# Normalised rows and squares in free PSUM banks, one root for the double norm, and the last chunks in token halves, in a two-block fp32 kernel on Trainium2

## The reference

```python
u = _modulate(h, g_ffn[l], sh2, sc2)                       # norm, scale, shift
h = h + gt2[:, None, :] * _conv_ffn(u, w_up[l], w_conv[l], b_conv[l], w_down[l])
return _rmsnorm(h, g_final)                                 # end of the first block
...
h = _rmsnorm_2(x, norm_g)                                   # start of the second
p = h @ w_in
(u, v, z_a, x_b, b_g, c_g, z_b, x_c, z_c, g_a, g_b, g_c) = jnp.split(p, _split_points(), axis=-1)
...
return x + merged @ w_o                                     # x is the once-normed row
```

## Time and profile before

| | us |
|---|---|
| median of 3 runs (lowest, highest) | 2197.65 (2197.61, 2199.75) |
| the profiled execution | 2197.53 |
| its span, first to last instruction | 2195.8 |
| outside the span | 1.7 |
| PE busy in the span | 2140.2 (97%) |
| DVE, ACT, POOL busy | 797.5, 415.8, 1048.4 |

### The profile page before, as it was taken

The page is one execution under the profiler, slowest core; times in us unless marked ns, Lnnn a source line. Parts: engine busy times, 40 slices in busy tenths (PEclk is TensorE's granted clock), DMA queues, the critical chain, the costliest instruction groups (busy, mean ns, idle before and its releaser), DMA issues.

```text
span 2195.8 us, 25443 instructions
## 1 busy us (share of the span) xinstructions
PE 2140.2 (97%) x10478; PEld 1782.1 (81%) x10478; DVE 797.5 (36%) x1072; ACT 415.8 (19%) x575; POOL 1048.4 (48%) x451
## 2 busy tenths in 40 slices
PE   7999999999999899999999989999999999999997
PEld 3788888888888788888888788888888888888885
DVE  6961355545543621222222674310031111331232
ACT  3202323233421310201111331111000110110102
POOL 1538447554453345445363525435545446435550
PEclk9999999999999999999999999999999999999999
DMA  9545554554451102011111221102111011101131
GB/s 347 118 101 153 192 149 144 155 153 136 167 182 39 39 31 85 29 48 48 48 58 29 87 106 58 38 30 67 58 39 48 29 58 58 48 29 58 38 124 77
DMA packets 157117, 192.26 MB, mean 88 GB/s; under 512 B 11152, under 2 KB 138720, under 8 KB 157024
## 3 DMA queue, kind: packets, MB, share of 16 engines
q1 hardware_dynamic: 148096, 172.05, 25.3%
q10 hardware_dynamic: 8928, 18.88, 2.3%
HBM read 159.20 MB, written 31.70 MB: 87 GB/s over the span
## 4 chain that ended last, share of the span: by engine, by line
PE 93%; DVE 3%; POOL 1%; DMA 1%; issue 1%; ACT 0%; SPq 0%; DVEq 0%; POOLq 0%; ACTq 0%
PE ps L718 62%; PE ps L792 8%; PE ps L740 8%; PE ps L750 4%; PE ps L1014 3%; PE ps L975 2%; PE ps L905 1%; PE ps L989 1%; DVE act_l L1797 1%; PE ps L1137 1%; POOL w_h L639 1%; DVE nrm L1786 1%; DMA ada_w<-in_w_ada 1%; PE ps L1242 1%; POOL w_l L641 1%
## 5 line engine op out<-in xcount | busy, mean ns | idle before, releaser
L639 POOL TENSOR_SCALAR w_h<-raw 128x1024 fp32r<-128x1024 f32 (+2 forms) x202 | 506.6, 2508 | 934.7 <-PE ps L718 595.5
L718 PE MATMUL ps<-act_h,w_h 128*128 128x512 f32 x1568 | 613.2, 391 | 1.0 <-POOL w_l L641 0.6
L718 PE MATMUL ps<-act_l,w_h 128*128 128x512 f32 x1568 | 610.6, 389 | 0.0
L718 PE MATMUL ps<-act_h,w_l 128*128 128x512 f32 x1568 | 610.6, 389 | 0.0
L641 POOL TENSOR_TENSOR w_l<-raw,w_h 128x1024 fp32r<-128x1024 f32 (+2 forms) x202 | 436.9, 2163 | 16.9
L718 PEld LDWEIGHTS ps<-act_h,w_h 128*128 128x128 f32 x1568 | 294.7, 188 | 65.9 <-issue 2.9
L718 PEld LDWEIGHTS ps<-act_h,w_l 128*128 128x128 f32 x1568 | 294.6, 188 | 61.4
L718 PEld LDWEIGHTS ps<-act_l,w_h 128*128 128x128 f32 x1568 | 294.8, 188 | 61.0 <-issue 0.5
L718 PE MATMUL ps<-in_h,w_h 128*128 128x512 f32 x384 | 150.3, 391 | 0.0
L718 PE MATMUL ps<-in_l,w_h 128*128 128x512 f32 x384 | 150.1, 391 | 0.0
L718 PE MATMUL ps<-in_h,w_l 128*128 128x512 f32 x384 | 150.1, 391 | 0.0
(11 more groups left out here) (325 smaller groups left out, 2824.2 us busy)
## 6 DMA issues: line engine op xcount, KB each, us to landing
raw<-in_w_in SPq DMA_DIRECT2D x45, 1024.0 KB, 5.2
raw<-in_w_up SPq DMA_DIRECT2D x16, 1024.0 KB, 5.5
ada_w<-in_w_ada SPq DMA_DIRECT2D x8, 1024.0 KB, 11.9
ada_lo<-in_w_ada SPq DMA_DIRECT2D x16, 512.0 KB, 3.9
ada_hi<-in_w_ada SPq DMA_DIRECT2D x16, 512.0 KB, 4.8
gates_scratch<-gate_st ACTq DMA_DIRECT2D x32, 256.0 KB, 2.5
gate_in<-gates_scratch SPq DMA_DIRECT2D x16, 512.0 KB, 4.5
raw<-in_w_down SPq DMA_DIRECT2D x16, 512.0 KB, 3.5
```

Source lines behind the costliest of these rows:

```text
L639: nc.gpsimd.tensor_scalar(w_h[:, k, c, :], src[:, c, :], 1.0, None, ALU.mult).then_inc(s["w_high"], 1)
L718: last = nc.tensor.matmul(dst[:, tok], w[:, k, kw + c, P * cg:P * cg + P], x[:, c, tok], start=(c == 0 and p == 0), stop=(c == kc - 1 and ...
```

## The change

**First norm.** The first half's sums go into the middle of u 0 (after its fourth input chunk), its spread into u 1 (after the third). The normalised rows' two buffers are now PSUM banks of slots 1 and 2, and the squares of chunks 4 to 7 are written into the PSUM banks from which the same chunk's product has just been read. ACT's root comes before the square of chunk 4's second half, and a dummy root (`root_table`) ahead of the squares. DVE does its second-half residuals and adds inside the loop of the first half's norm. The up-chunks go one at a time: slot 0, the second half's sums, slot 1 with the spread inside, slot 2, then slots 0, 1, 2 of the second half, and slot 3 whole.

**Double norm.** Four down chunks are whole and four (u 4 to 7) go in halves. ACT squares once, and the second sum is made on DVE by a multiply-add with `final_sq`. From both sums one root gives the product of the two reciprocals directly (`eps_sq`), and a second root, of the first norm alone, is spread later. The first half's sums stand after u 4 of the second half and its spread after u 5, with u 6 and u 7 behind it. The normalised rows go to PSUM banks (in the second half only the even chunks), and the squares of chunks 4 to 7 too. The first rows product of block two now takes one weight block at a time, with four token tiles per chunk; it waits until `sq_used` is past chunk 6's second half, since it overwrites the bank of that square. `scaled_out` comes behind both norms.

```diff
-        product_half(slot(u), 1 - u // 2, u % 2, KD, act_h, act_l, th)\
+        after = {}
+        if th and u == 0:
+            after[3] = lambda: statistics(acc, 7, slot(0)[:, 0:4], 0)
+        if th and u == 1:
+            after[2] = lambda: everywhere(2, slot(3)[:, 0:HALF], diag_a[:, 0]).then_inc(s["rstd_ready"], 1)
+        product_half(slot(u), 1 - u // 2, u % 2, KD, act_h, act_l, th, after=after)\
             .then_inc(s["gemm"] if th else s["first_half"], 1)
-        if th and u == 0:
-            statistics(acc, 7, slot(0)[:, 0:4], 0)
-        if th and u == 1:
-            everywhere(2, slot(3)[:, 0:HALF], diag_a[:, 0]).then_inc(s["rstd_ready"], 1)
...
-pair_half((0, 1), 1, 0, U_FFN, lambda: statistics(acc, 11, slot(2)[:, HALF:HALF + 4], 1))
-everywhere(3, slot(3)[:, HALF:T], diag_a[:, 1]).then_inc(s["rstd_ready"], 1)
+product_half(slot(0), 1, 0, KD, act_h, act_l, 0, each=s["u_ready"], base=U_FFN)
+statistics(acc, 11, slot(3)[:, HALF:HALF + 4], 1)
+product_half(slot(1), 1, 1, KD, act_h, act_l, 0, after={
+    4: lambda: everywhere(3, slot(3)[:, 0:HALF], diag_a[:, 1]).then_inc(s["rstd_ready"], 1)})
 split_done(N_FFN + 1)
-for cg in range(2):
-    product_half(slot(2 + cg), 0, cg, KD, act_h, act_l, 0)
-pair_half((0, 1), 1, 1, U_FFN + KD)
-for cg in range(2):
-    product_half(slot(2 + cg), 0, cg, KD, act_h, act_l, 1).then_inc(s["gemm"], 1)
+product_half(slot(2), 0, 0, KD, act_h, act_l, 0)
+product_half(slot(0), 1, 0, KD, act_h, act_l, 1, each=s["u_ready"], base=U_FFN + KD).then_inc(s["gemm"], 1)
+product_half(slot(1), 1, 1, KD, act_h, act_l, 1).then_inc(s["gemm"], 1)
+product_half(slot(2), 0, 0, KD, act_h, act_l, 1).then_inc(s["gemm"], 1)
+product(slot(3), 0, 1, KD, act_h, act_l).then_inc(s["gemm"], 1)
...
-down(None, 3, KD - 2)
+down(None, 3, 4)
 for th in range(2):
-    for u in (6, 7):
+    for u in range(4, KD):
+        n = 8 * 3 + N_FFN + 4 + u // 2
+            if u % 2 == 0:
+                pe.wait_ge(s["w_half"], n + 1)
+        product_half(slot(u % 4), 1 - (u // 2) % 2, u % 2, 4, in2_h, in2_l, th,
+                     rest=None if th or u % 2 else n).then_inc(s["gemm"] if th else s["first_half"], 1)
+        if th and u == 4:
+            both_sums(0, slot(0))
+        if th and u == 5:
+            spread(4, slot(1)[:, 0:HALF], diag_b[:, 0])
...
+pe.wait_ge(s["w_half"], N_V2 + 1)
+    if c == 0:
+        pe.wait_ge(s["sq_used"], SQ_DOWN + 4 * 2 * 2 + 5)
+    for t in range(4):
+        last = rows_tile(0, 0, t, c)
+    if c == 4:
+        both_sums(1, slot(3)[:, HALF:T])
+last.then_inc(s["gemm"], 1)
+split_done(N_V2 + 1)
+for t in range(4):
+    for c in range(KD):
+        last = rows_tile(0, 1, t, c)
+    if t == 0:
+        spread(6, slot(3)[:, HALF:T], diag_a[:, 0])
+        spread(5, slot(1)[:, 0:HALF], diag_b[:, 1])
+        spread(7, slot(1)[:, HALF:T], diag_a[:, 1])
+last.then_inc(s["gemm"], 1)
+pe.wait_ge(s["rstd1_read"], 2)
...
-    if c >= 3:
-        act.wait_ge(s["sq_used"], c + 2 if th and c >= 6 else c - 2)
-    A.activation(sq[:, c % 2, tok] if c else acc[:], h_t[:, c, tok], ACT.Square).then_inc(s["sq_ready"], 1)
+    if c == 3:
+        act.wait_ge(s["sq_used"], 1)
+    dst = acc[:] if c == 0 else sq[:, c % 2, :] if c < 4 else slot(c % 4)[:, tok]
+    A.activation(dst, h_t[:, c, tok], ACT.Square).then_inc(s["sq_ready"], 1)
...
+root_table()
 for c in range(4):
     square(c)
 for c in range(4, KD):
     square(c, 0)
+root(1, 0, slot(0)[:, 0:4])
 square(4, 1)
-root(1, 0, slot(0)[:, 0:4])
-square(5, 1)
-norm_high(U_FFN, slice(0, HALF), lambda i: nrm[:, i, 0:HALF], shift_ffn, lambda: square(6, 1))
+norm_high(U_FFN, slice(0, HALF), lambda i: slot(1 + i)[:, 0:HALF], shift_ffn,
+          {3: lambda: square(5, 1), 6: lambda: square(6, 1)})
 square(7, 1)
-root(2, 1, slot(2)[:, HALF:HALF + 4])
-norm_high(U_FFN + KD, slice(HALF, T), lambda i: nrm[:, i, HALF:T], shift_ffn)
+root(2, 1, slot(3)[:, HALF:HALF + 4])
+norm_high(U_FFN + KD, slice(HALF, T), lambda i: slot(1 + i)[:, HALF:T], shift_ffn)
...
+    act.wait_ge(s["down_read"], AHEAD + 24 + c + 1 + (4 if th else 0))
+    if c == 3:
+        act.wait_ge(s["sq_used"], SQ_DOWN + 3)
+    dst = acc2[:, 0, :] if c == 0 else sq[:, c % 2, :] if c < 4 else slot(c % 4)[:, tok]
+    A.activation(dst, h_t[:, c, tok], ACT.Square).then_inc(s["sq_ready"], 1)
...
+def roots(th):
+    cols = slice(4 * th, 4 * th + 4)
+    for m, (row, eps) in enumerate(((0, eps_sq), (3, eps_rms))):
+        act.wait_ge(s["ms2_ready"], 2 * th + 2)
+        A.activation(stat[:, row, cols], stat[:, 2 if m else 0, cols], ACT.Sqrt, scale=1.0 / D, bias=eps[:])\
+         .then_inc(s["std_ready"], 1)
...
+first_buf = [slot(1)[:, HALF:T], slot(3)[:, 0:HALF]]
+second_buf = [slot(3)[:, 0:HALF], sq[:, 1, 0:HALF]]
+root_table()
+for c in range(4):
+    square2(c)
+for c in range(4, KD):
+    square2(c, 0)
+square2(4, 1)
+roots(0)
+square2(5, 1)
+norm_high(U_IN2, slice(0, HALF), lambda i: first_buf[i], None,
+          {1: lambda: square2(6, 1), 3: lambda: square2(7, 1)})
+roots(1)
+norm_high(U_IN2 + KD, slice(HALF, T), lambda i: second_buf[i], None,
+          {1: lambda: keep_rstd(0, 6, slot(1)[:, 0:HALF]), 3: lambda: keep_rstd(1, 7, slot(1)[:, HALF:T])})
...
-    v.tensor_tensor(acc[:, tok], acc[:, tok], sq[:, c % 2, tok], ALU.add).then_inc(s["sq_used"], 1)
+    src = sq[:, c % 2, tok] if c < 4 else slot(c % 4)[:, tok]
+    v.tensor_tensor(acc[:, tok], acc[:, tok], src, ALU.add).then_inc(s["sq_used"], 1)
...
-residual(4, 1)
 one_over_root(2, slice(0, 4))
 on_diagonal(diag_a[:, 0], stat[:, 1, 0:4])
-residual(5, 1)
+residual(4, 1)
 add_square(4, 1)
 dve.wait_ge(s["rstd_ready"], 2)
-norm(U_FFN, slice(0, HALF), lambda i: nrm[:, i, 0:HALF], gain[:, 1], shift_ffn, slot(3)[:, 0:HALF], second_half)
+norm(U_FFN, slice(0, HALF), lambda i: slot(1 + i)[:, 0:HALF], gain[:, 1], shift_ffn, slot(3)[:, 0:HALF],
+     {2: lambda: residual(5, 1), 3: lambda: add_square(5, 1), 5: lambda: residual(6, 1), 6: lambda: add_square(6, 1)})
 residual(7, 1)
-add_square(6, 1)
 add_square(7, 1)
 one_over_root(3, slice(4, QB))
 on_diagonal(diag_a[:, 1], stat[:, 1, 4:QB])
 dve.wait_ge(s["rstd_ready"], 3)
-norm(U_FFN + KD, slice(HALF, T), lambda i: nrm[:, i, HALF:T], gain[:, 1], shift_ffn, slot(3)[:, HALF:T])
+norm(U_FFN + KD, slice(HALF, T), lambda i: slot(1 + i)[:, HALF:T], gain[:, 1], shift_ffn, slot(3)[:, 0:HALF])
...
-    for u in range(KD - 2 if last else KD):
+    for u in range(4 if last else KD):
+        if last and u == 1:
+            dve.wait_ge(s["sq_ready"], 13)
+            v.tensor_scalar(acc2[:, 1, :], acc2[:, 0, :], final_sq[:, 0:1], None, ALU.mult).then_inc(s["sq_used"], 1)
         if last and u >= 2:
             add_squares(u - 1)
...
+    n = c + (4 if th else 0)
+    src = sq[:, c % 2, tok] if c < 4 else slot(c % 4)[:, tok]
+    dve.wait_ge(s["sq_ready"], 12 + n + 1)
+    dve.wait_ge(s["sq_used"], SQ_DOWN + 2 * n - 1)
+    v.tensor_tensor(acc2[:, 0, tok], acc2[:, 0, tok], src, ALU.add).then_inc(s["sq_used"], 1)
+    v.scalar_tensor_tensor(acc2[:, 1, tok], src, final_sq[:, c:c + 1], acc2[:, 1, tok], ALU.mult, ALU.add)\
+     .then_inc(s["sq_used"], 1)
...
+def sums_out(th, src):
+    dve.wait_ge(s["sums_ready"], 4 + 2 * th)
+    v.tensor_copy(stat[:, 2, cols], src[:, 0:4]).then_inc(s["ms2_ready"], 1)
+    dve.wait_ge(s["ms2_ready"], 2 * th + 1)
+    v.scalar_tensor_tensor(stat[:, 0, cols], stat[:, 2, cols], RMS_EPS, src[:, 4:8], ALU.mult, ALU.add)\
+     .then_inc(s["ms2_ready"], 1)
+def both_diagonals(th, d):
+    cols = slice(4 * th, 4 * th + 4)
+    dve.wait_ge(s["std_ready"], 4 + 2 * th)
+    step(v.reciprocal(stat[:, 1, cols], stat[:, 0, cols]))
+    on_diagonal(d[:, 0], stat[:, 1, cols])
+    dve.wait_ge(s["std_ready"], 5 + 2 * th)
     step(v.reciprocal(stat[:, 4, cols], stat[:, 3, cols]))
-    step(v.tensor_tensor(stat[:, 5, cols], stat[:, 4, cols], r1, ALU.mult))
-    on_diagonal(d[:, 1], stat[:, 5, cols])
+    on_diagonal(d[:, 1], stat[:, 4, cols])
...
+step(v.tensor_tensor(gain2[:], col_b("g_final", 0, KD), col_b("norm_g_2", 0, KD), ALU.mult))
+step(v.tensor_tensor(final_sq[:], col_b("g_final", 0, KD), col_b("g_final", 0, KD), ALU.mult))
...
+residual2(4, 0)
+add_squares(3)
+for c in range(5, KD):
+    residual2(c, 0)
+    add_squares(c - 1, 0)
 add_squares(7, 0)
-residual2(6, 1)
-both_norms(0, 4, 4, slot(0)[:, HALF:HALF + 4], diag_b)
+residual2(4, 1)
+sums_out(0, slot(0))
+add_squares(4, 1)
+both_diagonals(0, diag_b)
+residual2(5, 1)
+add_squares(5, 1)
+dve.wait_ge(s["sq_used"], SQ_DOWN + 2 * 9 + 1)
+dve.wait_ge(s["rstd_ready"], 4)
+first_buf = [slot(1)[:, HALF:T], slot(3)[:, 0:HALF]]
+second_buf = [slot(3)[:, 0:HALF], sq[:, 1, 0:HALF]]
+norm(U_IN2, slice(0, HALF), lambda i: first_buf[i], gain2, None, slot(1)[:, 0:HALF],
+     {0: lambda: residual2(6, 1), 1: lambda: add_squares(6, 1),
+      2: lambda: residual2(7, 1), 3: lambda: add_squares(7, 1)})
+sums_out(1, slot(3)[:, HALF:T])
+both_diagonals(1, diag_a)
 dve.wait_ge(s["rstd_ready"], 5)
```

(9 more changed lines are left out.)

166 lines of the change are left out of this document (47 added, 119 removed).

## The result

| | before | after |
|---|---|---|
| median (lowest, highest), us | 2197.63 (2195.18, 2199.75) | 2179.51 (2174.77, 2180.25) |
| profiled execution, its span | 2197.53, 2195.8 | 2179.59, 2177.9 |
| PE busy in the span | 2140.2 (97%) | 2134.9 (98%) |

The ratio is 0.9913, with a 95% interval of 0.9896 to 0.9931: 18.1 us faster between the medians, where 19.3 were forecast.

The account below looks back on a forecast made before the run. PE, busy for 97% of the span, bounds the kernel, so only its idle and slow time can be won. Gains of 7.9 and 11.4 make 19.3 us off 2197.53: 2178.2, median 2178.3, range 2175.5 to 2181.5 (0.62).

Parts of the forecast that it names:

- The total: Both norms: gains of 7.9 and 11.4 make 19.3 us off the profiled execution, median 2178.3 us.
- First norm: First norm: 8.2 us of idle and slow PE time recovered, less a wait of 0.3, gains 7.9 us.
- Double norm: Double norm: 19.1 us recoverable, less new waits and slow clock of 1.3, 1.5, 0.15, 3.2 and 1.5, gains 11.4.
- 1.3 forecast for the weights: Double norm: PE idles 1.3 us for the weights of u 6 and 7, which POOL splits by 1236.6.
- 1.5 at the sums: Double norm, after u 4: PE idles 1.5 us before the sums, until DVE's adds are done at 1245.1.
- 3.2 ahead of the rows product: Double norm: PE idles 3.2 us until chunk 6's adds free the square's bank; slow clock then costs 1.5 us.
- Rival (a): Double norm: clock also falls in the two gaps before the sums, 8 us apart; 2181.5 to 2185, chance 0.14.
- PSUM operands: DVE in both norms: PSUM operands taken at equal price, 0.75 us; up to 0.1 more each would give 2181.
- rival (d): Both norms, slower: scalings that write PSUM and read their factor there cost 1.1 us extra each; 2204, chance 0.03.
- Rival (b): Both norms: POOL still stops DVE, the cause not being the second SBUF input; gains 2.5 and 9, 2186, chance 0.09.
- a DVE operation does not stand still for a TENSOR_SCALAR: DVE beside POOL: operations with both inputs in SBUF stall for POOL's TENSOR_TENSOR only; `act_l` beside a `w_h` took 0.75.
- The table load: First norm: the 1.28 us load moves ahead of the squares; root, reciprocal and diagonal then end at 698.6.

Follow-up runs that it names:

- rows_in_sbuf: Changed kernel with the buffers of the normalised rows back in SBUF in both norms, squares and order as changed: 2188.15 us, 8.6 above the changed kernel.
- combined_late: Changed kernel with the edits of squares23_psum and square6_sbuf, plus chunk 6's and 7's adds and the second sums two chunks later: 2174.76 us, again 2175.91.
- squares23_psum: Changed kernel with the squares of chunks 2 and 3 of the double norm also in PSUM: 2175.69 us, ratio 0.99.
- the probes: Changed kernel with idle gaps and sums put into PE's stream in block two, alone, paired or together; one profiled execution, no total time given.
- square6_sbuf: Changed kernel with the second half of chunk 6's square in SBUF, not in the bank the rows product overwrites: 2180.01 us, ratio 0.9919.
- no_early_table: Changed kernel without the two dummy roots ahead of the squares, in both norms: 2177.95 us, ratio 0.9908.
- first_norm_only: Kernel before the change with only the first norm's hunks, its double norm as it was: 2190.82 us, ratio 0.9967.
- double_norm_only: Kernel before the change with only the double norm's hunks, its first norm as it was: 2186.95 us, ratio 0.9948.
- combined_v2: combined_late with the first half's sums one input chunk later and chunk 6's second residual ahead of the third scaling: 2174.0 us, ratio 0.9892.

## Why the prediction was right, point by point

**The total** holds: 19.3 us forecast for the two norms, 8.35 + 10.95 = 19.3 measured. That the two agree to a tenth is luck: the gaps of the double norm came out 1.2 us shorter than forecast, and a slow stretch of 1.7 us that the sum did not have came in. (The list of waits has a line of 6.5 us between the two that I read as the longest; it is PE's wait for the input at the start, outside the norms.)

**First norm, 7.9 forecast, 8.35 measured.** The steps came as drawn: sums inside u 0, spread 5.7 us after them, no stall in `act_l`, the second half's adds ready at 720.91 where PE reached the sums at 724.19, so 3.3 us of slack. I had put a wait of 0.2 to 0.3 at chunk 7 of the second half; there is none: the norm's last `act_l` ends at 741.39, and PE runs through. `rows_in_sbuf` shows that the PSUM buffers carry 6.2 of the 8.35.

**Double norm, 11.4 forecast, 10.95 measured.** The gaps: 1.3 forecast for the weights (its terms, 1236.6 and 1235.4, give 1.2), 0.86 measured; 1.5 at the sums, 1.19 measured (each chunk's residual and adds repeat after 1.92 us, not 1.98); 0.15 at the spread, none measured; 3.2 ahead of the rows product, 2.86 measured. Behind that gap the clock fell as forecast. The term that was missing is the slow clock at the sums: from their start to the next matmul it took 2.11 us (1237.64 to 1239.75) and the 12 matmuls behind took 4.14 (to 1243.89), where 1.80 (`combined_late`, 1236.09 to 1237.89) and 2.72 are the prices at the upper level: 1.7 us lost. Rival (a), with a chance of 0.14, had such a loss at 1.5 to 3.5. Its total of 2181.5 to 2185 did not come, since the gaps made up for most of it: 4.91 us against the 6.15 forecast. Its reason, that two gaps lie 8 us apart, is not borne out: in `squares23_psum` the first gap is gone and the clock fell at the sums, and the probes' pair of gaps left it at 1.00.

**PSUM operands** cost nothing, as taken: 0.76 against 0.75 for a scaling into PSUM, 0.68 for an add from PSUM and 0.68 for one from SBUF (before, at 683.47), and ACT's square into PSUM takes 0.60 where it took 0.63 into SBUF. That excludes rival (d). The rule of the Trainium skill, "VectorE: DVE Perf Modes", section on the TRN2 errata, on a dearer PSUM source, is not seen here.

**Rival (b)**, that POOL stops DVE for another reason, is excluded by `rows_in_sbuf`, `square6_sbuf` and `squares23_psum`: one input moved to SBUF brings 0.74 up to 2.9, one input moved to PSUM takes 2.3 down to 1.28. In all thirteen profiles 127 SCALAR_TENSOR_TENSOR of 512 columns with an input in PSUM began under a `w_l`, and none took over 0.76; the ten with SBUF inputs only took 2.11 to 2.92. It also bears on the second rule that I weighed. The Trainium skill, "SBUF — State Buffer", section "Who interferes with whom", has any GpSimd instruction that reads SBUF block a DVE instruction with two SBUF inputs. A `w_h` did not hold up the `act_l` at 708.90 (0.75), nor that `act_l` the `w_h` around it (2.77). POOL pays in another place: the `w_h` of 713.29 begins while the stalled `act_l` of 711.02 is still finishing, and takes 3.22.

But the prediction's sentence that a DVE operation does not stand still for a TENSOR_SCALAR is too wide. In block two of after the same operation, with both inputs in SBUF, took 1.94 us inside a `w_h` and 1.22 beside none, and that `w_h` took 3.75 instead of 2.77:

```profile
1356.16 1.94 DVE L2260 TENSOR_TENSOR a_s<-a_s,a_z 128x1024 f32<-128x1024 f32 x1
...
1364.94 1.22 DVE L2260 TENSOR_TENSOR a_s<-a_s,a_z 128x1024 f32<-128x1024 f32 x1
```
```profile
1355.01 3.75 POOL L643 TENSOR_SCALAR w_h<-raw 128x1024 fp32r<-128x1024 f32 x1
```

In the thirteen profiles 251 such wide TENSOR_TENSOR with SBUF inputs lie wholly inside a `w_h`; 98 of them took over 1.31 us, and 83 of these 98 inside a `w_h` that was itself longer than 3 us. Within the norms it mattered little: the `act_l` there kept 0.75. So the rule holds in part for a TENSOR_SCALAR as well, and what decides is open.

**The table load** did stand in the first norm's chain before: it ran from 700.70 to 701.98, behind a square, while the sums were over at 699.94. The forecast took it off by the dummy root. `no_early_table` shows that the new place of the real root does that alone, so the number was right for a wrong reason.

**The medians** moved by 1.2 us less than the sum. The profiles lose 1.36 ahead of w_out, at the place told below. Whether the medians lose it there as well no trace tells, since only one execution of each run is traced. Two series of after against before gave 18.1 and 18.9 us, so a difference of this size can also be the spread of the runs.

## What to carry to other kernels

When DVE work lies beside POOL's two-input operations, give each DVE operation one operand in PSUM, even if that is only a temporary buffer in a bank that is free for the moment; it speeds up POOL too. Look for what else still reads SBUF alone after such an edit: one forgotten add under a `w_l` took 1 to 2 us longer each time, and moving two of them won 1.5 us on the path (`squares23_psum`). A gap on PE that DVE's chain sets closes by moving work that no one waits for (here the adds of the last chunks) behind work that PE waits for, and such a gap is worth closing for its own length. Whether that also saves slow clock cannot be counted on: at the double norm's sums 1.7 us were lost behind gaps of 1.19, 0.83 and 0.16 us, and nothing behind 0.84.

## What I had not expected of the hardware

**The clock falls without idle time.** Near 108 us PE does 64 matmuls of 64x16 in 4.5 us, back to back, and the clock falls to 0.50 in twelve of the thirteen profiles while PE is busy all the time. After, and then `no_early_table`, in which it did not happen:

```profile
108.00:112.00 4.00, 4.00 (x45) 3.77 (x44) 0.78 (x2) 0.52 (x2) 3.92 (x3) 0.66 0.90 205
112.00:116.00 4.00, 4.00 (x11) 3.13 (x10) 3.93 (x3) 0.00 (x0) 3.92 (x2) 0.50 0.28 32
```
```profile
112.00:116.00 4.00, 4.00 (x19) 3.32 (x18) 3.93 (x3) 0.10 (x1) 3.92 (x2) 1.00 0.28 35
```

The same instructions lost 0, 1.7 (before, `first_norm_only`, `double_norm_only`, `combined_v2`) or 3.4 us (after and all others). This is the largest difference between kernels ahead of the first norm, and it is no effect of the change: but for one more memset the code there is the same, and kernels with the double norm's change show all three values. A comparison of two profiled spans has to leave such a stretch out, as the table above does.

**A slow stretch has few sizes.** At this place and in the two norms of all thirteen profiles the losses were multiples of about 1.7 us, whatever the gap: 1.7 behind 2.9 us idle, 3.4 around 6 us idle, 5.1 (before) or 3.4 (`first_norm_only`) around the same 5.17, 1.7 or 3.4 at sums with 1.2 us idle ahead of them, 1.7 or nothing with 0.83 or 0.84, and 1.7 with 0.16. What makes the clock fall at the sums is not shown: the probes with a gap of 0.72 ahead of sums did not reproduce it.

**The table load hides itself** if the root is next in ACT's order. In `no_early_table` it starts as soon as ACT reaches the root (1235.52), 2 us before the root's input is there. In before's first norm a square stood ahead of the root, and the load came behind it, in the chain.
